# Counting a norm's statistics steps double when the steps of three mixes are spread over the slots

## What is computed

```
h = x @ w_in                      # q | k | v | u, 512 columns each
a = stick_breaking_attention(q, k, v)          # 8 heads of 64
p = pooled_differences(u) @ pool_w             # 4 trailing windows
x1 = LayerNorm(ALPHA * x + concat[a, p] @ w_out)        # "the mix" and the first norm
y  = LayerNorm(ALPHA * x1 + (silu(x1 @ w_gate) * (x1 @ w_up)) @ w_down)
```

## Time and profile before

| | |
|---|---|
| median of 3 runs | 2617.8 us (2615.91 to 2618.01) |
| the profiled execution, time | 2616.77 us |
| the profiled execution, span | 2614.9 us |
| PE busy | 2536.8 us, 97% of the span |
| DVE busy | 1574.0 us, 60% |
| ACT busy / POOL busy | 1153.8 us / 1169.6 us |
| mean granted TensorE clock | 0.995 |

### The profile page before, as it was taken

One profiled execution on the slowest core, in us unless ns is written; L12 is line 12 of the kernel. 1 busy time (PEld: TensorE's weight loads), 2 busy tenths in 40 slices (PEclk: granted clock), 3 DMA queues, 4 the chain that ended last, 5 costly groups with the idle time before them and its releaser, 6 DMA issues.

```text
span 2614.9 us, 37788 instructions
## 1 busy us (share of the span) xinstructions
PE 2536.8 (97%) x13994; PEld 2164.0 (83%) x13994; DVE 1574.0 (60%) x2127; ACT 1153.8 (44%) x1932; POOL 1169.6 (45%) x1030
## 2 busy tenths in 40 slices
PE   8999999999999999999999999999999999999998
PEld 8978798788878988778788887878878887889997
DVE  3266336666434357787744477787775355867766
ACT  4366326565232135566531265656554213343333
POOL 3465436755223135456631174556653214344444
PEclk9999999999999999999999999999999999999999
DMA  6697956774446233444354244333533522233322
GB/s 228 191 273 249 332 178 193 227 216 125 134 132 234 81 113 109 117 120 110 89 188 154 97 121 117 101 109 103 150 99 107 205 65 89 73 105 107 96 95 85
DMA packets 211015, 373.93 MB, mean 143 GB/s; under 512 B 30768, under 2 KB 105136, under 8 KB 208784
## 3 DMA queue, kind: packets, MB, share of 16 engines
q1 hardware_dynamic: 210832, 371.50, 45.6%
HBM read 303.34 MB, written 68.09 MB: 142 GB/s over the span
## 4 chain that ended last, share of the span: by engine, by line
PE 82%; DVE 6%; issue 3%; DMA 3%; POOL 2%; ACT 2%; SPq 1%; POOLq 0%; ACTq 0%; DVEq 0%
PE bank L1284 27%; PE bank L1346 19%; PE bank L1234 8%; PE bank L1193 7%; PE bank L1292 7%; PE bank L1093 5%; PE bank L1140 4%; PE bank L1109 4%; DMA gw_lo_raw<-in_w_in_dram 2%; DVE left L1902 1%; POOL gw_lo L2548 1%; PE bank L1216 1%; DMA v_st<-v_cache_scratch 1%; DVE acc L1941 0%; DMA mixT<-mixT_scratch 0%
## 5 line engine op out<-in xcount | busy, mean ns | idle before, releaser
L1284 PE MATMUL bank<-x1T,gw_hi 128*128 128x512 f32 (+1 forms) x2336 | 713.4, 389 | 4.8 <-DVE hT_lo_raw L2004 3.4
L2478 POOL TENSOR_TENSOR beta<-beta,left 128x512 f32<-128x512 f32 (+2 forms) x326 | 349.7, 1073 | 359.7 <-DVE left L1902 359.0
L1284 PEld LDWEIGHTS bank<-x1T,gw_hi 128*128 128x128 f32 x2336 | 419.3, 189 | 85.1 <-issue 4.5
L1284 PE MATMUL bank<-x1T,gw_lo 128*128 128x512 f32 (+1 forms) x1168 | 448.2, 384 | 0.0
L1902 DVE TENSOR_TENSOR_SCAN left<-bank,left,zero_t 128x512 f32<-128x512 f32 (+2 forms) x326 | 363.9, 1116 | 75.2 <-ACT bank L1469 69.4
L2505 POOL TENSOR_TENSOR gw_lo<-gw_lo_raw,gw_hi 128x1024 fp32r<-128x1024 f32 x70 | 181.8, 2597 | 427.5 <-ACT gw_hi L1536 427.3
L1234 PE MATMUL bank<-x1T,gw_hi 128*128 128x256 f32 (+2 forms) x1472 | 355.7, 334 | 13.0 <-DVE x1T L2266 8.8
L1459 ACT ACTIVATE aT<-bank 128x512 fp32r<-128x512 f32 (+2 forms) x326 | 173.7, 533 | 434.0 <-PE bank L1109 384.6
L2179 DVE TENSOR_TENSOR acc<-bank,acc 128x512 f32<-128x512 f32 x312 | 213.3, 686 | 215.2 <-PE bank L1346 212.1
L1893 DVE TENSOR_TENSOR aT<-bank,aT 128x512 fp32r<-128x512 f32 (+2 forms) x326 | 196.9, 604 | 202.7 <-ACT aT L1459 201.5
L1346 PE MATMUL bank<-dw_hi,hT_hi 128*128 128x512 f32 x728 | 296.0, 407 | 9.7 <-issue 7.2
(11 more groups left out here) (226 smaller groups left out, 4655.2 us busy)
## 6 DMA issues: line engine op xcount, KB each, us to landing
gw_lo_raw<-in_w_gate_dram SPq DMA_DIRECT2D x88, 512.0 KB, 3.6
gw_lo_raw<-in_w_up_dram SPq DMA_DIRECT2D x88, 512.0 KB, 3.9
dw_lo_raw<-in_w_down_dram SPq DMA_DIRECT2D x86, 512.0 KB, 4.4
gw_lo_raw<-in_w_in_dram SPq DMA_DIRECT2D x64, 512.0 KB, 4.5
k_st<-kT_scratch SPq DMA_DIRECT2D x160, 128.0 KB, 4.2
v_st<-v_scratch SPq DMA_DIRECT2D x80, 256.0 KB, 4.4
q_st<-qT_scratch SPq DMA_DIRECT2D x128, 128.0 KB, 4.1
wo_raw<-in_w_out_dram SPq DMA_DIRECT2D x16, 1024.0 KB, 5.7
```

The lines of the kernel that those rows point to most:

```text
L1284: m = pe.matmul(gu_bank(g, n)[:, 0:w], gw[L % 4][a][:, k, :], x1T[x][:, k, first:first + w], start=k == 0 and s == 0, stop=k == KD - 1 and ...
L2478: pool.tensor_tensor(x[:, 0:w], x[:, 0:w], left[n % RL][:, 1:w + 1], ALU.mult).then_inc(a_done, 1)
```

## The change

One line of `spread`: a step of mix 1, 2 or 3 weighs 2 instead of 1 from `stats_step` on. Attention steps keep their weights, and so do mix 0, the ends of the stretches and the norms' slots.

```
     def spread(ticks, first, end):
-        weights = [1 if k != ATTENTION or g != SAMPLE_BLOCK else 7 if SAMPLE_AT - 1 <= s <= SAMPLE_AT + 4
+        weights = [1 + (g > 0 and s >= stats_step(g)) if k == MIX else 1 if g != SAMPLE_BLOCK else 7 if SAMPLE_AT - 1 <= s <= SAMPLE_AT + 4
                    else 2 if SAMPLE_AT + AT_V - 1 <= s <= SAMPLE_AT + AT_V + 5 else 1 for k, g, s in ticks]
```

## The result

The changed kernel takes 2622.04 us in the median (2618.72 to 2628.66, 13 runs), the kernel before, beside it, 2615.91 us (2612.55 to 2622.19, 13 runs). The ratio is 1.0025, with a 95% interval of 1.0017 to 1.0032: slower by 6.1 us in the medians, between 4.4 and 8.4 by the interval. The forecast was 1.1 us faster. The chance of slower by over 0.2% had been set at 0.08.

The account below looks back on a forecast made before the run. TensorE, busy 97% of the span, was taken as the bound, so only its gaps could move. Mixes of -0.15, +2.38 and -3.3 sum to -1.1 us: from the median 2617.8 to 2616.7 us, range 2613.5 to 2621.2.

Parts of the forecast that it names:

- Mix 1, -0.15: Mix 1: PE's 1.57 us wait for VectorE's times_gate goes, a 1.42 us wait before down piece d6 comes; -0.15 us.
- Mix 2, +2.38: Mix 2: the 0.81 us times_gate wait goes, waits of 1.77 before d3 and 1.42 before d7 come; +2.38 us.
- the rival of a fall in mix 2: Mix 2: the lower clock follows the new 1.77 us gap, price 1.53 us, total 2618.2 us; chance 0.20.
- Mix 3, the gap ahead of d0 and its clock, -4.07: Mix 3, before down piece d0: PE's 2.54 us wait for VectorE's split and 1.53 us of lower clock go.
- One loss of 1.5 us is hidden by the 2 us, a second is not; I leave 0.3 us of gap for it.: Mix 3: allowance for GpSimd lengthening VectorE's centrings by 1.5 us each; 0.3 us of gap left, so 3.77 gained.
- The 2 us: Mix 3: VectorE's spare time before PE reaches d0, 14.6 us of work against PE's arrival at 16.8.
- The 1.53 us of clock: Mix 3, behind the 2.54 us gap: nine matmul starts took 3.64 instead of 2.11 us at half clock; expected back.
- The rival with two losses: Mix 3: two GpSimd delays keep PE waiting for the split, 2.2 us gap plus 1.5 of clock, 2620.1 us; chance 0.07.
- The first product, 0.5: Mix 3: the first product, four pieces earlier, waits 0.5 us for wo_lo and the last mixT load, between 0.4 and 3.2.
- The 1.44 us for `gw_lo`: Mix 3, at 2185: PE's 1.44 us gap stays, since it hangs on GpSimd's queue behind norms in unmoved slots.
- Nothing else beside these mixes stops PE for longer than 0.1 us: Ends of the three mixes: only gaps of 1.57, 0.81, 2.54 and 1.44 us, so at most 6.4 us to gain.
- The sentence on the Trainium skill's rule: Mix 3: shared VectorE/GpSimd ports make each overlap cost up to a whole GpSimd instruction; gap about 1 us, gain 3.1.

Follow-up runs that it names:

- the kernel with slots of its own: Before's order, but VectorE's statistics and centrings of mixes 1 to 3 get separate slots, mix 3's sample-tile fold and centring behind times_gate: 2615.30 us, ratio 0.9991.

## Why the prediction was wrong

- **Mix 1, -0.15: right** (-0.29 and -0.30 in two kernels). The gap of 1.57 went, and the one at d6 was 1.31 instead of 1.42.
- **Mix 2, +2.38: right** (+2.34 and +2.35). The rule that a piece waits for the add two pieces back gave 1.77 and 1.42, and the rows show gaps of 1.62 and 1.31. The time lost is as forecast even so: the last matmul of d2 starts at 1496.33 and d3 at 1498.35, 2.02 us later where matmuls follow each other every 0.23, so 1.79 us are lost. The gap of the row is shorter because it counts from the end of that matmul, whose row lasts 0.39 us. The clock stayed at 1.00 behind these gaps in all five traces that have them, so the rival of a fall in mix 2 did not come true; that it could have is possible, since behind a gap of 1.64 us in the attention (at 773.91, in the kernel with slots of its own) the clock did fall.
- **Mix 3, the gap ahead of d0 and its clock, -4.07: that gap went as forecast, the gain did not come.** The step that failed is "One loss of 1.5 us is hidden by the 2 us, a second is not; I leave 0.3 us of gap for it." There were three losses that PE had to wait for, of 2.16, 2.19 and 2.03 us, and the gap was 3.42 us instead of 0.3. The 1.53 us of clock did not come back either, since the new gap brought the lower clock in all three traces of after. The losses' size was taken from one centring that met a split some 0.8 us old; one that starts just behind the start of a split waits for nearly all of its 2.4 us. Their number was taken as small because the splits' rows of before were not carried over to the new order: the change leaves GpSimd's own order alone, and in after two centrings and the copy stand beside its splits.
- **The slack was read at the wrong reader.** The 2 us were counted to `times_up` and the split of line 2165, on which before's gap hung. The delays fell ahead of `times_gate` of the same chunk, for which PE comes four pieces sooner; there 3.0 us of 6.4 were hidden. The rival with two losses had the right mechanism, but its price was 2.2 us of gap and 1.5 us of clock, and its chance 0.07.
- **The first product, 0.5: the mechanism was right, the size was 0.7 to 1.0.** It is again the last `mixT` load.
- **The 1.44 us for `gw_lo` stayed**, as forecast, and its reason was right: moving the norms took it away. The prediction's "Nothing else beside these mixes stops PE for longer than 0.1 us" passes over the 0.83 us ahead of the transposes at the end of mix 3; they stand in every trace and so change nothing here.
- **The sentence on the Trainium skill's rule** gave a gap of about 1 us and was nearer than the 0.3 that was used, but it too counted with too few meetings.
- **The range** ended at 2621.2 and the time was 2622.04. The forecast for mix 3 was off by 5.8 us on the mean of three traces (+2.5 against -3.3), out of the 7.2 us between the medians' +6.1 and the forecast's -1.1; the rest is the 1.5 us left open above.

## What to carry to other kernels

When steps of VectorE are moved, lay their new places against GpSimd's timeline, not only against VectorE's own: an operation of 1.2 us grew to 3.4 where it started just behind a GpSimd instruction, and two of these with a copy that grew from 0.7 to 2.7 turned a gain into a loss. Count the slack at each wait of the engine that bounds, one after the other, since work that leaves one wait lands ahead of the next. A table of weights moves everything at once; giving the few operations places of their own, where the trace showed both engines idle, brought 0.27% where the doubled weights cost 0.25%.

## What the runs showed of the hardware

- GpSimd's two-input instruction from SBUF held up VectorE's centring (two inputs) and its copy of 32x1024 with one input: 1.23 to 3.39 us, and 0.69 to 2.72. It works in the other direction too: the split of 2160.61 took 3.33 us instead of 2.41 behind a centring that ended at 2161.73. With one operand in PSUM nothing of this showed: in before's trace the add of line 2179 at 2164.04 took 0.69 us in the middle of 8 us of GpSimd's norm steps.
- The granted clock behind a gap of PE cannot be read off its length: behind 3.42 us it fell in four traces of five, behind one wait of 1.75 us it was 0.50 in one and 1.00 in another, and behind a wait of 2.53 us in the attention (at about 1076 us) it fell in thirteen traces of fourteen. In mix 3 it then stood at 0.50 for 3.4 us, which held the matmuls back by 1.5 us, and once for 6.8 us, which held them back by 2.8. The prediction had looked for a bound between 1.73 and 1.86 us in one trace; there is none: it fell behind 1.64 us in the kernel with slots of its own and did not behind 2.53 and 3.42 us in two others.
